# Second block's input projection continued inside the first feed-forward stage, first chunk by token halves, last down weights in their own buffers

## The reference

```python
gate, up = jnp.split(xn @ w_gate_up[l], 2, axis=-1)
x = x + (jax.nn.silu(gate) * up) @ w_down[l]        # end of the first block
return rms_norm(x, final_norm_g)
...
h = rmsnorm(x, w_norm_mix[l])                       # start of the second block
proj = h @ w_mix_in[l]                              # 1024 x 3592
(sc_b, sc_c, sc_h, gq, gk, gv, gz, ga, gb, sq, sk, sv) = split_columns(proj)
...
g = -jnp.exp(gdn_a_log) * jax.nn.softplus(ga + gdn_dt_bias)   # 4 columns; gb 4 more
```

## Time and profile before

| | |
|---|---|
| median of 3 runs | 2899.94 us (2898.33 to 2902.72) |
| the profiled execution's own time | 2911.94 us |
| its span | 2910.2 us |
| PE busy | 2737.7 us (94%) |
| DVE / POOL / ACT busy | 1298.7 / 1175.2 / 663.5 us |
| mean granted clock of PE | 0.971 |

### The profile page before, as it was taken

How to read it: one execution, slowest core, us unless ns; L and a number is a source line. 1 busy time by engine, 2 the same in 40 slices (tenths; PEclk the granted TensorE clock), 3 DMA queues, 4 the chain that set the end, 5 groups by cost and what they waited for, 6 DMA issues and landing times. The chain is left out here.

```text
span 2910.2 us, 34840 instructions
## 1 busy us (share of the span) xinstructions
PE 2737.7 (94%) x12979; PEld 2189.7 (75%) x12979; DVE 1298.7 (45%) x1808; ACT 663.5 (23%) x1244; POOL 1175.2 (40%) x919
## 2 busy tenths in 40 slices
PE   4999887999999999989999888889999999999998
PEld 2888446888888888866888677774588888888876
DVE  4032541423334333462351356667334555566667
ACT  2010561210001000151132233345322121111123
POOL 2443026234444444523454323330323555455552
PEclk9999998999999999999999889999999999999999
DMA  3110103111111111211111000000311111111111
GB/s 103 46 50 26 40 15 130 30 38 50 43 50 48 49 50 47 65 73 44 48 49 49 1 1 1 1 16 1 112 33 33 51 47 44 50 47 50 50 55 72
DMA packets 91081, 131.61 MB, mean 45 GB/s; under 512 B 9333, under 2 KB 57696, under 8 KB 90984
## 3 DMA queue, kind: packets, MB, share of 16 engines
q1 hardware_dynamic: 88680, 121.88, 13.8%
q10 hardware_dynamic: 2304, 8.39, 0.7%
HBM read 121.82 MB, written 8.42 MB: 45 GB/s over the span
## 5 line engine op out<-in xcount | busy, mean ns | idle before, releaser
L123 POOL TENSOR_TENSOR w_hi<-w_raw,zero 128x512 fp32r<-128x512 f32 x344 | 406.3, 1181 | 1076.2 <-PE bank L1002 450.3
L125 POOL TENSOR_TENSOR w_lo<-w_raw,w_hi 128x512 fp32r<-128x512 f32 x344 | 497.8, 1447 | 26.9
L1000 PE MATMUL bank<-xt_hi,w_hi 128*128 128x512 f32 x1248 | 485.7, 389 | 1.6 <-DVE x_sb L1210 0.8
L1001 PE MATMUL bank<-xt_lo,w_hi 128*128 128x512 f32 x1248 | 485.5, 389 | 0.0
L1002 PE MATMUL bank<-xt_hi,w_lo 128*128 128x512 f32 x1248 | 485.5, 389 | 0.0
L1308 DVE TENSOR_TENSOR x_sb<-bank,x_sb 128x512 f32<-128x512 f32 x320 | 221.3, 692 | 202.9 <-PE bank L1036 202.5
L1000 PEld LDWEIGHTS bank<-xt_hi,w_hi 128*128 128x128 f32 x1248 | 234.2, 188 | 51.1 <-DVE x_sb L1210 1.3
L1002 PEld LDWEIGHTS bank<-xt_hi,w_lo 128*128 128x128 f32 x1248 | 234.2, 188 | 48.7
L1001 PEld LDWEIGHTS bank<-xt_lo,w_hi 128*128 128x128 f32 x1248 | 234.2, 188 | 48.6
L177 PE MATMUL bank<-xt_hi,w_hi 128*128 128x512 f32 x512 | 199.4, 390 | 0.0
L177 PE MATMUL bank<-xt_lo,w_hi 128*128 128x512 f32 x512 | 199.2, 389 | 0.0
(11 more groups left out here) (448 smaller groups left out, 4811.3 us busy)
## 6 DMA issues: line engine op xcount, KB each, us to landing
w_raw<-in_w_gate_up_dram SPq DMA_DIRECT2D x88, 256.0 KB, 3.1
w_raw<-in_w_ffn_up_dram SPq DMA_DIRECT2D x88, 256.0 KB, 3.1
w_raw<-in_w_mix_in_dram SPq DMA_DIRECT2D x56, 256.0 KB, 2.7
w_raw<-in_w_down_dram SPq DMA_DIRECT2D x44, 256.0 KB, 2.6
w_raw<-in_w_ffn_down_dram SPq DMA_DIRECT2D x44, 256.0 KB, 2.7
w_raw<-in_w_in_dram SPq DMA_DIRECT2D x40, 256.0 KB, 2.7
x_sb<-in_x_dram SPq DMA_DIRECT2D x8, 512.0 KB, 6.3
gate_rows<-gate_sums SPq DMA_DIRECT2D x8, 512.0 KB, 4.8
```

Source lines behind the costliest of these rows:

```text
L123: pool.tensor_tensor(m.w_hi[:, u, :], m.w_raw[:, u, :], zeros, ALU.add).then_inc(m.hi_done, 1)
L125: pool.tensor_tensor(m.w_lo[:, u, :], m.w_raw[:, u, :], m.w_hi[:, u, :].bitcast(F32), ALU.subtract).then_inc(m.split, 1)
L1000: pe.matmul(m.psum[b][:, :], u_hi[:, col], m.xt_hi[:, k, tok], start=k == 0, stop=False)
L1001: pe.matmul(m.psum[b][:, :], u_hi[:, col], m.xt_lo[:, k, tok], start=False, stop=False)
```

## The change

Four things are moved or added. (1) In both feed-forward stages the last group's down weights are split into `end_hi`, `end_lo` rather than into `w_hi`, `w_lo`, and wait for the last up products alone. (2) The eight banks of the transposition become four; the first half's transposes come right behind the last down product, ACT's and DVE's parts of them are spread over the last tiles by `turns_at`, and the second half's transposes stand between products. (3) The barrier goes: the second projection's program is called inside the block. Its chunk 0 is done for tokens 0 to 511 (banks 4 to 7), then for 512 to 1023 (banks 0 to 3), slices 4 to 7 out of `end_hi`, `end_lo`. (4) The gate products follow chunk 0, and the gate columns are transposed in chunk 2.

```diff
-    spare = [m.at(f"scaled_out{i}" + tag, [P, 4, D], (16, 152)[i]) for i in range(2)]
-    junk = m.at("mlp_squares" + tag, [P, 4, D], 176)
+    spare = [m.at(f"scaled_out{i}" + tag, [P, 4, D], (16, 176)[i]) for i in range(2)]
+    junk = m.at("mlp_squares" + tag, [P, 2, D], 0)
...
         @block.gpsimd
...
-            split_slices(m, pool, last + 12, DN)
-            if first is not None:
-                pool.wait_ge(scl, 2 * NT)
-                split_first(m, pool, base + 16 + 12 * FI)
+            for u in range(DN):
+                n = last + 12 + u
+                pool.wait_ge(m.used, last + RING + u + 1)
+                pool.wait_ge(m.loaded[u], 16 * (n // RING) + 16)
+                pool.tensor_tensor(end_hi[:, u, :], m.w_raw[:, u, :], zeros, ALU.add).then_inc(m.hi_done, 1)
+                pool.wait_ge(m.hi_done, n + 1)
+                pool.tensor_tensor(end_lo[:, u, :], m.w_raw[:, u, :], end_hi[:, u, :].bitcast(F32),
+                                   ALU.subtract).then_inc(m.split, 1)
+            if nxt is not None:
+                nxt.gpsimd(pool)
...
-                    down_bank(last_hi, last_lo, (2 * t + nh) % NB, t, nh, dn_done)
-            if next_gcol is not None:
-                for n in range(2 * KD):
-                    h, k = n // KD, n % KD
-                    if k == 0:
-                        pe.wait_ge(scl, NT + 4 * (h + 1))
-                        pe.wait_ge(dn_ev, 16 * FI + NB)
-                    if n >= NB:
-                        pe.wait_ge(t_lo, 16 + n + 1 - NB)
...
+                    down_bank(last_hi, last_lo, (2 * t + nh) % NB, t, nh, dn_done, end_hi, end_lo)
+            def turn_next(h, k):
+                n = KD * h + k
+                pe.wait_ge(scl, NT + 4 * (h + 1))
+                if n < 4:
+                    pe.wait_ge(dn_ev, 16 * (FI - 1) + NB + 8 + n + 1)
+                else:
+                    pe.wait_ge(t_lo, 16 + n - 3)
+                for j in range(4):
+                    mm = pe.transpose(m.psum[n % 4][:, j * P:(j + 1) * P], spare[h][:, j, k * P:(k + 1) * P], m.ident[:, :])
+                mm.then_inc(turned, 1)
+            if nxt is not None:
+                for k in range(KD):
+                    turn_next(0, k)
+                nxt.tensor(pe, turn_next, t_lo, dn_ev)
...
+        turns_at = {NT - 2: (0, 1), NT - 1: (2, 3), NT: tuple(range(4, 2 * KD))}
...
             for t in range(NT + 1):
...
-            if next_gcol is not None:
-                for n in range(2 * KD):
+                for n in turns_at.get(t, ()) if nxt is not None else ():
                     h, k = n // KD, n % KD
                     act.wait_ge(turned, 16 + n + 1)
...
+            if nxt is not None:
+                act.wait_ge(stored, 16 * NT)
+                nxt.scalar(act)
...
                     rescale(t - 2)
+                for n in turns_at.get(t, ()) if nxt is not None and t < NT - 1 else ():
+                    low(16 + n, n % 4, next_gcol)
             normed(NT - 1)
-            if next_gcol is not None:
+            if nxt is not None:
                 rescale(NT - 2)
+                for n in turns_at[NT - 1]:
+                    low(16 + n, n % 4, next_gcol)
                 rescale(NT - 1)
...
+                for n in turns_at[NT]:
+                    low(16 + n, n % 4, next_gcol)
+                nxt.vector(dve)
...
+    def gpsimd(pool):
...
+        for u in range(RING):
+            n = base + u
+            pool.wait_ge(m.used, n + 1 - 2 * RING)
+            split_slice(m, pool, n, n // RING, u, True)
+        for u in range(RING):
+            n = base + RING + u
+            pool.wait_ge(m.used, n + 1 - 2 * RING)
+            pool.wait_ge(m.loaded[u], 16 * (n // RING) + 16)
+            pool.tensor_tensor(nxt.hi[:, u, :], m.w_raw[:, u, :], zeros, ALU.add).then_inc(m.hi_done, 1)
...
+    def tensor(pe, turn, t_lo, dn_ev):
...
+        for h in range(2):
+            tok = slice(h * HALF, (h + 1) * HALF)
+            for k in range(KD):
...
+                pe.wait_ge(m.split, base + k + 1)
+                pe.wait_ge(t_lo, 16 + 8 * h + k + 1)
+                for n in range(4):
+                    bank, col = m.psum[4 + n - 4 * h], slice(n * P, (n + 1) * P)
+                    if k == 0 and h == 0:
+                        pe.wait_ge(dn_ev, nxt.dn + 4 + n + 1)
+                    if k == 0 and h:
+                        pe.wait_ge(t_lo, 16 + 13 + n)
...
+                if h == 0 and 3 <= k < 7:
+                    turn(1, 2 * (k - 3))
+                    turn(1, 2 * (k - 3) + 1)
+        pe.wait_ge(f_split, 2)
+        for h in range(2):
+            pe.wait_ge(evac, h + 1)
...
+                if c == 2 and b == 3:
+                    gate_columns()
```

More of the change, by code:

```diff
@@ L840, in paired_first, with mlp_stage @@
     return lambda u: (m.w_raw[:, u, :], w[(u // 2) * P:(u // 2 + 1) * P, (u % 2) * HALF:(u % 2 + 1) * HALF])
[L843 removed]
+def mlp_stage(m, tag, w_out, scales, load_x, gcol, w_up, w_down, x_sb, conv, gain, store, next_gcol=None, nxt=None):
     nc = m.nc
@@ L875, in mlp_stage @@
     GU, DN = 8, 4
+    if nxt is not None:
+        nxt.follow(base + 16 + 12 * FI, c0 + FI, 16 * (FI - 1) + NB + 8, end_hi, end_lo)
     def place(n):
@@ L1602, in proj2_stage, with follow, load_first @@
-    m.slices += 8 * NC
-    m.chunks += NC
+    def follow(base, c0, dn, hi, lo):
+        nxt.base, nxt.c0, nxt.dn, nxt.hi, nxt.lo = base, c0, dn, hi, lo
+    def load_first(sp):
+        sp.dma_start(wf[:, :, :], w[:, 2816:2824].rearrange("(k p) n -> p k n", p=P)).then_inc(in_small, 16)
+        for k in range(KD):
+            u = k % RING
+            sp.wait_ge(m.split, nxt.base + k + 1 - RING)
+            sp.dma_start(m.w_raw[:, u, :], w[k * P:(k + 1) * P, 0:HALF]).then_inc(m.loaded[u], 16)
@@ L1606 @@
+    nxt.follow, nxt.load_first = follow, load_first
+    nxt.sync, nxt.gpsimd, nxt.tensor, nxt.scalar, nxt.vector = sync, gpsimd, tensor, scalar, vector
+    nxt.slices, nxt.chunks = 8 * NC, NC
+    return nxt
 SBD = 64
```

365 lines of the change are left out of this document (189 added, 176 removed).

## The result

The changed kernel takes 2881.09 us, median of 6 runs (2878.92 to 2889.98); the kernel before, in the same session, 2900.41 us, median of 6 (2898.33 to 2907.93). The ratio is 0.9932, 95% interval [0.9915, 0.9948]: faster, by 0.7%. The forecast was 2884.2 us, a ratio of 0.9946. Applied to the 2899.94 us shown before, the measured ratio gives 2880.2 us, 4 us under the forecast and just under the lower end of its range. So the sign came as forecast, and so did the mechanism in the places touched, but the gain was larger: 19 to 20 us where 15.7 were worked out, of which 17.2 lie in those places.

A forecast was written before the change was run, and what follows sets the result against it. PE was taken to bound the kernel, so only its waits and slow stretches could give time back. 10.7 + 5.05 = 15.7 us took 2911.94 to 2896.2, less 12 us to the median: 2884.2 us, range 2881 to 2890.

The forecast's parts named there:

- Part 1: Last down product, both feed-forward stages: PE starts 3.35 us earlier, 1.7 us of slow matmuls go, 5.05 us each.
- the second stage gains nothing: Second feed-forward stage: DVE, slowed by moved splits, replaces the removed wait; 2889.3 us, chance 0.08.
- Part 2: Tiles behind the last down product: DVE waits for ACT at `low(0)`, contention costs 1.0 us, chunk 0's products begin at 1301.8.
- The two `normed` at 0.9, less their cover: DVE's last tiles beside POOL's splits: contention costs 1.0 us, from two `normed` steps, `rescale` not counted.
- the upper bound of 2.3: Same tiles: contention costs 2.3 us if `normed(6)`, `rescale(5)`, `normed(7)` and `rescale(6)` are each held up by 0.9.
- signs of being wrong: PE waiting for a split in chunk 0, second-half banks waiting for ACT, `normed` at 2 us, slow stretch over 5 us.
- Part 3: Chunk 0 by halves with transposes inside, then gates: chunk 1 begins at 1362.6 instead of 1373.28, 10.7 us earlier.
- PE was nearly idle for 13 us, so the clock is low at the start: I take the 2.3 us: Start of chunk 0: slow matmuls cost 2.3 us, taken from an earlier 7.5 us wait; bounds 1.7 and twice 2.3.
- The clock doesn't fall: Start of chunk 0: transposes keep the clock up, the 2.3 us aren't lost; 2881.9 us, chance 0.06.
- the forecast's own upper bound of 17.3: Whole kernel: largest gain of the forecast, 15.7 + 1.0 + 0.6 = 17.3 us, giving 2882.6 us.
- The median, 2899.94, stands 12 us under it, and I take the same difference off: Last step, whole kernel: the profiled execution's predicted 2896.2 us less 12 us gives a median of 2884.2 us.

The follow-up runs named there:

- e2: The changed kernel with the second feed-forward stage's last down weights split into `w_hi` and `w_lo` as before: 2885.68 us, ratio 0.9944 to the kernel before.
- e3: The changed kernel with POOL's splits of the projection's slices 4 to 7 held back until DVE's last `rescale`: 2875.85 us, ratio 0.9908 to the kernel before.
- e4: The changed kernel with all sixteen `xt_hi`/`xt_lo` behind the last tile's steps: 2882.48 us, ratio 0.9927 to the kernel before.
- e5: The changed kernel with turns 6 and 7 of the transposes behind the products of k = 3: 2881.75 us, ratio 0.993 to the kernel before.
- e7: The changed kernel with turns 6 and 7 behind the products of k = 3 and late POOL splits of slices 4 to 7: 2884.43 us, ratio 0.993.
- e1: The kernel before with only the last down weights split into `end_hi` and `end_lo`, both stages, two buffers moved: 2888.23 us, ratio 0.9948.
- e11: e5 with eight useless repeats of the recurrence stage's first product ahead of it: ratio 0.9972 to the kernel before.

## Where the prediction held, and the step that failed

The time is 4.0 us under the forecast. 1.5 of them lie in the places touched, where one term of the sum was taken too large, the low clock at the start of chunk 0; the other 2.5 come from the last step, which leaves out the stages behind the change, and these take the time out of the range.

- **Part 1** held: waits of 0.83 instead of 4.18 and 4.17 us, over 0.1 us after DVE's last read (1262.84 + 0.69), no slow matmuls behind them, 5.1 us in the second stage (e2) against 5.05. The rival that the second stage gains nothing fell.
- **Part 2** came out at 36.5 us where 36.0 were worked out. "The two `normed` at 0.9, less their cover" was right in sum (1.0 by e3) and wrong in its parts: `rescale`, counted as not held up, took 1.53 and 1.76 us instead of 0.75, while of the two `normed` behind the wait the first took 1.60 us and the second, with no split beside it, 1.27. The Trainium skill, page SBUF — State Buffer, section "Who interferes with whom", had counted `tensor_scalar` among those that are held up; the trace agrees with it on this, 1.53 and 1.76 us beside the splits and 0.76 without (e3). Its sum, the upper bound of 2.3, did not come, because the splits were over before the last two tiles. One of the signs of being wrong did show, a `normed` of 2 us (2.24), but under the cover of the wait.
- **Part 3**: "PE was nearly idle for 13 us, so the clock is low at the start: I take the 2.3 us" is the term that was mis-sized. Three slow products cost 0.7 us. The clock was low ahead of them: the eight transposes took 1.59 us to the next start where they take 0.92 at the higher one. So 0.7 of the cost fell into the transposes, which the sum had at 0.46 for each bank, and 0.7 into the products. A part of the first 0.7 is why the products begin at 36.5 us and not at 36.0: from the end of `low(3)` (1297.66 + 1.40) to the first product it takes 1.1 us, not 0.46. Everything else of part 3 fits: chunk 0 takes 47.9 us, that is 43.8 + 3.4 for the transposes inside + 0.7, and the gates 11.1. The two waits with slow matmuls behind them were no measure of this one: eleven or twelve were slow there. The rival "The clock doesn't fall" has a time, 2881.9, that is nearer to the measured one than the forecast's; but the clock did fall, to 0.50 from 1291.3 to 1301.5, and that nearness is luck.
- **Sum of the places touched**: 17.2 us in place of 15.7, just inside the forecast's own upper bound of 17.3. With it alone the time would be 2882.7 us, inside the range of 2881 to 2890.
- **The step that failed** is "The median, 2899.94, stands 12 us under it, and I take the same difference off". It puts at nothing, without a reason, what stages with the same code gain or lose. They didn't keep their time: the recurrence stage went from 192.7 or 199.7 to 191.1 us, the column to ffn2 from 23.1 to 20.6, together 4.1 us between the second profiles and 11.2 between the first. Against the medians some 2.5 us are missing, and that carries the time out of the range. The 2.5 us to ffn2 are clock too. In both kernels PE waits 3.5 us there and starts the products with the output weights 9.6 us behind the last product of the stage before; before, the clock has fallen by then and thirteen of them start 0.36 to 0.57 us apart; after, it has not fallen and all but the first start 0.23 apart. Windows from 4 to 16 us behind that stage's last product, in which PE is busy 8.50 us in both; kernel before, second profile:

```profile
2060.60:2068.60 8.00, 4.50 (x24) 0.77 0.18 39
2068.60:2072.60 4.00, 4.00 (x13) 0.61 1.01 396
```

Changed kernel, second profile:

```profile
2045.50:2053.50 8.00, 4.50 (x28) 1.00 0.13 38
2053.50:2057.50 4.00, 4.00 (x19) 1.00 1.02 390
```

- **Open**: why the clock falls and comes back where it does in those stages. That the course differs is shown, and that it repeats to 0.1 us in two profiles of the changed kernel (and in e2) while the kernel before showed two courses. The courses don't go with the change as such: the column to ffn2 is short in the change, e2, e4, e5 and e7, but long in e3 (23.2), which has all of the change, and the shortest recurrence stages are those of e1 and e3. What goes with the recurrence stage's length in the profiles is how far behind its first product the clock first falls: 3.6 us in e1 and e3 (188.1 both), 2.9 in the change, its repeat and e2 (191.1), 2.6 and 2.7 in e5 and e7 (197.4, 197.8). But 1.9 gave 192.0 (e4), and 1.4 and 1.3 in the kernel before gave 199.7 and 192.7, so that alone doesn't decide either. Whether the change brings the shorter course by when it reaches these stages or by what PE did before them was not separated.

## What to carry to other kernels

A wait of PE that goes because weights have buffers of their own is worth the wait and the slow matmuls behind it (5.1 us in e2), and both could be read from the rows before. An idle stretch of DVE beside a POOL that is splitting can be cover: with it filled (e4), contention fell onto steps that had none. And a gain in front of a stage whose granted clock goes up and down should be read at the stage's door, over two profiles of each kernel, before the end-to-end time is believed: e5 arrived 6.6 us earlier and ended no earlier.

## What the runs showed of the hardware

- After an idle stretch slow matmuls are those that fall into what is left of a low stay of the clock: in the change it ends at 1301.5 us, 1.4 behind the first product (three slow), in e4 at 1300.0, 0.3 ahead of it (none). Their number did not follow the length of the wait: none behind 0.83 us; 11 and 12 behind 4.18 and 7.5 us; 3 behind the 5.8 us of the change, the clock being low through the eight transposes ahead; 6 in the same place in e3, behind 4.9 us, with the low stay ending 2.7 us behind the first product; 5 in e5, whose products begin behind a wait of 3.5 us; none in e4, behind a wait of 11.4 us, whose sixteen transposes took 3.0 us there instead of 1.9.
- The clock also falls while PE is busy without a break: in the recurrence stage, 1.3 to 3.6 us behind its first narrow product (8x512) in all fourteen profiles, within 0.1 us of the same point in the two profiles of the kernel before and in the two of the change. It then stays at 0.50 for 3.4 us (e1, e3) to 17.1 us (before), and for 27 us behind the eight added products of e11.
- DVE and POOL slow each other in both directions: DVE's `TENSOR_SCALAR` of 128x1024 goes from 0.75 us to 1.53 and 1.76, its `SCALAR_TENSOR_TENSOR` of 128x1024 from 1.28 to 2.24, POOL's splits of 128x512 from 1.04 to 2.02 and from 1.27 to 2.13. DVE steps that read a bank (`low` 1.41 us for two, `last_down` 1.28 for two) and the splits beside them (1.03, 1.27 us) keep their durations.
